# A hybrid decoder layer on one core: inputs turned by the host layout, FFN 1 first, memory keys and values beside the cross-attention

## The reference

```python
h = rmsnorm(x, ffn1_norm);  x = x + 0.5 * swiglu(h, ffn1_w_gate, ffn1_w_up, ffn1_w_down)   # 2048 -> 5504 -> 2048
h = rmsnorm(x, mix_norm);   proj = h @ w_in          # latent attention and gated recurrence on its columns
x = x + concat([a, r]) @ w_out
h = rmsnorm(x, xattn_norm); m = rmsnorm(mem, mem_norm)
x = x + memory_xattn(h, m, xattn_w_q, xattn_w_kv, xattn_q_norm, xattn_k_norm, xattn_w_o)
h = rmsnorm(x, ffn2_norm);  x = x + 0.5 * swiglu(h, ffn2_w_gate, ffn2_w_up, ffn2_w_down)

def memory_xattn(h, m, w_q, w_kv, q_norm, k_norm, w_o):      # 4 heads of 128
    q = rmsnorm((h @ w_q) per head, q_norm)
    kv = (m @ w_kv) per head;  k = rmsnorm(first 128 columns, k_norm);  v = last 128 columns
    p = softmax(q @ k.T * 128 ** -0.5)
    return (p @ v) @ w_o
```

## Time and profile before

| | |
|---|---|
| median of 3 runs | 2006.64 us (2006.51 to 2006.73) |
| profiled execution, first to last instruction (its span) | 2003.2 us; the profile gives no other time of its own |
| median less span: what lies around the instructions | 3.4 us |
| PE busy / DVE / ACT / POOL | 98% / 50% / 42% / 5% of the span |
| weight slots through `w_hi` | 341 |
| data moved | 357.89 MB, 179 GB/s on the mean |
| mean granted TensorE clock | 0.995 of full speed |

### The profile page before, as it was taken

One profiled execution on the slowest core, in us unless ns is written; L12 is line 12 of the kernel. 1 busy time (PEld: TensorE's weight loads), 2 busy tenths in 40 slices (PEclk: granted clock), 3 DMA queues, 4 the chain that ended last, 5 costly groups with the idle time before them and its releaser, 6 DMA issues. The chain is left out here.

```text
span 2003.2 us, 21967 instructions
## 1 busy us (share of the span) xinstructions
PE 1955.2 (98%) x9138; PEld 1635.0 (82%) x9138; DVE 999.3 (50%) x784; ACT 850.3 (42%) x795; POOL 100.1 (5%) x79
## 2 busy tenths in 40 slices
PE   7999999999999999999998998999999999999999
PEld 6888888888888988898886776788888888888987
DVE  4644444444444455475656564544444444444443
ACT  5533333333333334554546445444333333433332
POOL 0100000000000000150324000000000000000000
PEclk9999999999999999999999998999999999999999
DMA  8555555555555655555543353355555555555653
GB/s 311 168 191 190 189 190 189 191 197 194 189 188 163 210 179 184 158 168 168 168 147 107 104 168 126 113 192 190 190 190 191 191 191 189 190 189 173 198 190 131
DMA packets 182430, 357.89 MB, mean 179 GB/s; under 512 B 6500, under 2 KB 17111, under 8 KB 182103
## 3 DMA queue, kind: packets, MB, share of 16 engines
q1 hardware_dynamic: 182358, 356.88, 54.4%
HBM read 354.76 MB, written 2.10 MB: 178 GB/s over the span
## 5 line engine op out<-in xcount | busy, mean ns | idle before, releaser
L875 DVE TENSOR_TENSOR w_lo<-w_raw,w_hi 128x2048 fp32r<-128x2048 f32 (+1 forms) x341 | 772.7, 2266 | 911.1 <-ACT w_hi L524 910.0
L524 ACT ACTIVATE w_hi<-w_raw 128x2048 fp32r<-128x2048 f32 (+1 forms) x341 | 640.6, 1879 | 1011.9 <-PE acc L1370 1011.4
L1368 PE MATMUL acc<-w_hi,hT_hi 128*128 128x512 f32 (+2 forms) x1760 | 680.0, 386 | 0.8 <-DVE w_lo L875 0.8
L1370 PE MATMUL acc<-w_lo,hT_hi 128*128 128x512 f32 (+2 forms) x1760 | 675.8, 384 | 0.0
L1369 PE MATMUL acc<-w_hi,hT_lo 128*128 128x512 f32 (+2 forms) x1760 | 675.3, 384 | 0.0
L1368 PEld LDWEIGHTS acc<-w_hi,hT_hi 128*128 128x128 f32 x1760 | 330.5, 188 | 64.5 <-issue 3.2
L1370 PEld LDWEIGHTS acc<-w_lo,hT_hi 128*128 128x128 f32 x1760 | 330.4, 188 | 63.0
L1369 PEld LDWEIGHTS acc<-w_hi,hT_lo 128*128 128x128 f32 x1760 | 330.6, 188 | 61.0
L1368 PE MATMUL acc<-w_hi,actT_hi 128*128 128x512 f32 x752 | 295.5, 393 | 4.7 <-DVE w_lo L875 4.7
L1370 PE MATMUL acc<-w_lo,actT_hi 128*128 128x512 f32 x752 | 293.3, 390 | 0.0
L1369 PE MATMUL acc<-w_hi,actT_lo 128*128 128x512 f32 x752 | 293.3, 390 | 0.0
(11 more groups left out here) (204 smaller groups left out, 907.0 us busy)
## 6 DMA issues: line engine op xcount, KB each, us to landing
w_raw<-in_ffn_w_gate SPq DMA_DIRECT2D x80, 1024.0 KB, 5.1
w_raw<-in_ffn_w_up SPq DMA_DIRECT2D x80, 1024.0 KB, 5.1
w_raw<-in_ffn_w_down SPq DMA_DIRECT2D x80, 1024.0 KB, 5.2
w_raw<-in_w_in SPq DMA_DIRECT2D x36, 1024.0 KB, 5.1
w_raw<-in_w_out SPq DMA_DIRECT2D x16, 1024.0 KB, 5.2
w_raw<-in_xattn_w_kv SPq DMA_DIRECT2D x8, 1024.0 KB, 11.4
w_raw<-in_ffn_w_gate SPq DMA_DIRECT2D x8, 768.0 KB, 4.4
w_raw<-in_ffn_w_up SPq DMA_DIRECT2D x8, 768.0 KB, 4.4
```

Source lines behind the costliest of these rows:

```text
L524: nc.scalar.activation(w_hi[:, c % SPLIT, 0:n], raw[:, c % RAW, 0:n], ACT.Copy).then_inc(hi_done, 1)
L875: v.tensor_tensor(w_lo[:, c % SPLIT, 0:n], raw[:, c % RAW, 0:n], w_hi[:, c % SPLIT, 0:n].bitcast(F32), ALU.subtract).then_inc(lo_done, 1)
L1368: mm(dst, xh, wh, start=first and kk == 0, stop=False)
L1370: ins = mm(dst, xh, wl, start=False, stop=last and kk == tiles - 1)
```

## The change

- The host lays out more: `x` and `mem` come turned as well (`x_turned`, `mem_turned`), the norm gains as columns (`gain_columns`), and `xattn_w_kv` as two weights, keys (`xattn_w_k`) and values (`xattn_w_v`). PE no longer turns `mem`, `x` and the gains; ACT and DVE make the two parts straight from the loaded data.
- FFN 1 comes first. Its first slot is loaded, split and multiplied in four pieces of one k-tile (`first_slots`, `first_piece`).
- The 8 slots on the memory move: 4 key slots (`mem_k`) ahead of `w_q`, where they now take the place between which the norm of `x` is worked off; 4 value slots (`mem_v`) between the steps of the cross-attention. `mem` turned is loaded in two halves into one buffer (`load_memT`), which SP does in the midst of the loads of `w_out`, and split behind M5 and M7 (`mem_turned`).
- In the cross-attention the second scaling of the queries is gone: their 1/rms goes into the exponential's scale and the maxima, and POOL multiplies once more.
- The angles and bounds and the square sums of `mem` move into FFN 1's first down product.

```diff
@@ SP
+            def load_first():
+                sp.dma_start(gains[:, 0:N_ROWS], a["gain_columns"]).then_inc(gains_in, 16)
+                for k in range(4):
+                    sp.dma_start(xT[:, k, :], a["x_turned"][:, k, :]).then_inc(xT_in[k], 16)
+                    sp.dma_start(raw[:, 0, k * NW:(k + 1) * NW], wg[k * P:(k + 1) * P, 0:NW]).then_inc(first_in[k], 16)
+                for s in range(1, 4):
+                    sp.dma_start(xT[:, 4 * s:4 * s + 4, :], a["x_turned"][:, 4 * s:4 * s + 4, :]).then_inc(xT_in[3 + s], 16)
+                    load(s, 0, rows_of(wg, 4 * s, 4, slice(0, NW)), 4, NW)
...
+                        if n == "w_out" and j == 2 and s == 0:
+                            sp.wait_ge(ev("o_scaled"), 1)
+                            load_memT(0)
+                        if n == "w_out" and j == 3 and s == 0:
+                            sp.wait_ge(m_lo, KD // 2)
+                            load_memT(1)
                         load(slots[n] + 2 * j + s, 0, rows_of(a["w_out"][0], k0 + 4 * s, 4, slice(j * NW, (j + 1) * NW)), 4, NW)
-            for s in range(4):
-                load(slots["xq"] + s, 0, rows_of(a["xattn_w_q"][0], 4 * s, 4, slice(0, NW)), 4, NW)
+            for n, w in (("mem_k", a["xattn_w_k"]), ("xq", a["xattn_w_q"][0]), ("mem_v", a["xattn_w_v"])):
+                for s in range(4):
+                    load(slots[n] + s, 0, rows_of(w, 4 * s, 4, slice(0, NW)), 4, NW)
@@ ACT and DVE, behind M5 and M7 (ACT: hi and mT_hi; DVE: lo, add_block and mT_lo)
+                if k in (5, 7):
+                    mem_turned(k // 2 - 2)
@@ ACT
             for s in range(4):
                 hi(slots["xq"] + s, 0, 4, NW)
                 if s == 0:
+                    take(blocks["mem_k"], slots["mem_k"] + 4, lambda t: memk_nat[:, t, :], ACT.Copy, cols(rsq, "mem"))
+            turned(memkT, 0, groups["memk"], gain=col["xattn_k_norm"])
+            hi(slots["mem_v"], 0, 4, NW)
...
+            x_exps(0)
+            hi(slots["mem_v"] + 2, 0, 4, NW)
+            x_prob_turned(0)
+            x_exps(1)
+            hi(slots["mem_v"] + 3, 0, 4, NW)
+            x_prob_turned(1)
+            hi(slots["w_o"], 0, 4, NW)
+            take(blocks["mem_v"], slots["mem_v"] + 4, lambda t: memv[:, t, :], ACT.Copy, cols(rsq, "mem"))
+            hi(slots["w_o"] + 1, 0, 4, NW)
@@ DVE
+            x_shift(0)
+            lo(slots["mem_v"] + 2, 0, 4, NW)
+            x_shift(1)
+            lo(slots["mem_v"] + 3, 0, 4, NW)
             for p in range(XH // 2):
                 dve.wait_ge(ev("x_exps"), p + 1)
                 done(v.reciprocal(srec[:, p, :], ssum[:, p, :]))
+            lo(slots["w_o"], 0, 4, NW)
+            lo(slots["w_o"] + 1, 0, 4, NW)
             done.wait()
@@ PE
+            values_slot(0)
+            pe.wait_ge(ev("xq_raw"), TT)
+            turn_features(groups["xq"], 0, of(gate))
+            values_slot(1)
+            split_stands(groups["xq"])
+            x_scores(0)
+            values_slot(2)
+            x_scores(1)
+            x_probs(0)
+            values_slot(3)
+            x_probs(1)
+            stands(blocks["mem_v"])
```

More of the change, by code:

```diff
@@ L380, in load_memkv @@
[L380 to L392, removed]
@@ L508, in _ @@
             norm("k")
-            for name in ("o_mla", "x3", "xq", "x4"):
+            for name in ("o_mla", "x3", "memk"):
                 norm(name)
+            norm("xq", X_SCALE)
+            norm("x4")
         @block.scalar
@@ L552, in square_sums @@
                     done.wait()
-                    ins = nc.scalar.activation(flat_stage[:, 0:src.shape[2]], src[:, t, :], ACT.Square, accum_out=cols(sums, name, t, 1))
+                    junk = flat_stage[:, 0:src.shape[2]] if name != "mem" else src[:, t, :]
+                    ins = nc.scalar.activation(junk, src[:, t, :], ACT.Square, accum_out=cols(sums, name, t, 1))
                     if t == 0:
@@ L601, in pair @@
                         ins.then_inc(acc_taken[b0 % 2], 1)
-                        if not prev and h == 0 and f == 1:
-                            turned(memkT, 0, groups["memk"], gain=col["xattn_k_norm"])
-                        hi(c + 6, rep, 4, width)
-                        hi(c + 7, rep, 4, width)
+                        if not first:
+                            hi(c + 6, rep, 4, width)
+                            hi(c + 7, rep, 4, width)
                     pair(0, 0)
@@ L850, in _, with x_prob_turned @@
                 act.sem_inc(ev("x_exps"), 1)
-            for p in range(XH // 2):
+            def x_prob_turned(p):
                 for t in range(TT):
@@ new lines, in x_turned, with mem_turned @@
+            def x_turned(k):
+                c = col["ffn1_norm"] + k
+                dve.wait_ge(x_hi, k + 1)
+                v.scalar_tensor_tensor(hT_lo[:, k, :], xT[:, k, :], gains[:, c:c + 1], hT_hi[:, k, :].bitcast(F32),
+                                       ALU.mult, ALU.subtract).then_inc(x_lo, 1)
+            def mem_turned(half):
+                for k in range(KD // 2):
+                    c = half * KD // 2 + k
+                    g = col["mem_norm"] + c
+                    dve.wait_ge(m_hi, c + 1)
+                    v.scalar_tensor_tensor(mT_lo[:, c, :], memT[:, k, :], gains[:, g:g + 1], mT_hi[:, c, :].bitcast(F32),
+                                           ALU.mult, ALU.subtract).then_inc(m_lo, 1)
@@ L1288, in _ @@
                     turned_lo(hT_hi, hT_lo, 4 * (k // 2 - 2), groups["x_out"] + k // 2 - 2, 0, splits["x_out"] + k // 2 - 2, 0, gain=col["xattn_norm"])
+                if k in (5, 7):
+                    mem_turned(k // 2 - 2)
+            for s in range(4):
+                lo(slots["mem_k"] + s, 0, 4, NW)
+                if s == 0:
+                    turned_lo(hT_hi, hT_lo, 4 * (DB - 2), groups["x_out"] + DB - 2, 0, splits["x_out"] + DB - 2, 0, gain=col["xattn_norm"])
+                entry("x3", s, slots["mem_k"])
@@ L1355, in of, with slot @@
                 return lambda m, t: src[:, t, col0 + m * P:col0 + (m + 1) * P]
-            def slot(c, rep, B, lhs_hi, lhs_lo, k0, tiles, width, first, last, off=0, full=None, signal=True):
-                pe.wait_ge(lo_done, c + rep + 1)
+            def slot(c, rep, B, lhs_hi, lhs_lo, k0, tiles, width, first, last, off=0, full=None, signal=True, pieces=None):
+                if pieces is None:
+                    pe.wait_ge(lo_done, c + rep + 1)
                 full = full or width
                 for kk in range(tiles):
+                    if pieces is not None:
+                        pieces(kk)
                     w0 = kk * full + off
@@ L1642, in _ @@
                         turn_features(groups["x_out"] + j - 1, 0, of(x, (j - 1) * NW))
+            B = blocks["mem_k"]
+            free(B)
+            for s in range(4):
+                pe.wait_ge(m_lo, 4 * s + 4)
+                slot(slots["mem_k"] + s, 0, B, mT_hi, mT_lo, 4 * s, 4, NW, s == 0, s == 3)
+                entry("x3", s)
             B = blocks["xq"]
@@ L1648, in _, with values_slot, x_scores @@
                 slot(slots["xq"] + s, 0, B, hT_hi, hT_lo, 4 * s, 4, NW, s == 0, s == 3)
-                entry("x3", s)
-            pe.wait_ge(ev("xq_scaled"), 1)
-            turn_features(groups["xq"], 0, of(gate))
-            split_stands(groups["xq"])
-            for p in range(XH // 2):
+            pe.wait_ge(ev("memk"), 1)
+            turn_features(groups["memk"], 0, of(memk))
+            def values_slot(s):
+                B = blocks["mem_v"]
+                if s == 0:
+                    free(B)
+                slot(slots["mem_v"] + s, 0, B, mT_hi, mT_lo, 4 * s, 4, NW, s == 0, s == 3)
+            def x_scores(p):
                 for t in range(TT):
```

368 lines of the change are left out of this document (188 added, 180 removed).

## The result

| | before | after |
|---|---|---|
| median | 2006.68 us (2006.51 to 2006.96) | 2030.83 us (2028.9 to 2031.29) |
| ratio | | 1.012, interval 1.0107 to 1.0132 |
| span of the profiled execution | 2003.2 us | 2027.0 us |

The change costs 24 us. The prediction was 2022.6, range 2012 to 2030: the sign and all three waits were right, the size was 8 us short, and the time lies 0.8 us above the range.

The account below looks back on a forecast made before the run. PE, busy 98% of the span, was taken as the bound. Start -9.6, keys' turn -1.0, M6 +8.9, key slots +0.3, cross-attention +12.2, clock +5.2 sum to +16.0: span 2019.2, plus 3.4 gives 2022.6 us, range 2012 to 2030.

Parts of the forecast that it names:

- all three waits: Forecast case, chance 0.70: slower, with PE waiting at slot 1, before M6 and in the cross-attention.
- T to `w_o`: Cross-attention, end of fourth `w_q` slot to first `w_o` matmul: 61.3 us at full clock; 12.2 us lost.
- the clock's term: Waits of 8.9, 6.2 and 6.9 us before M6, v2, v3 each restart PE's clock: 3 x 1.75 = 5.2 us.
- With those of 5.1 and 3.8 it would be 8: Upper end for clock restarts: counting also the waits before v0 and the outputs, 8 us.
- the clock holds at 2.4 GHz: Rival, chance 0.08: PE's clock stays at 2.4 GHz through the waits, giving 2017 us.
- the value slots cover the waits: Rival, cross-attention at v2 and v3, chance 0.07: splits run under PE's previous slot, 12 us gained, 1995 us.
- SP's wait: Before M6: its load stands behind `mem`'s second half, which waits on `m_lo`; PE waits 8.9 us.
- not late: Rival before M6, chance 0.08: loads behind SP's wait are under way beside M5; no 8.9 us wait, 2012 us.
- Start: FFN 1's beginning: first matmul at 7.2 us, slot 1 at 17.7 after a 3.3 us wait; gain 9.6 us.
- Slot 1 4 us later: FFN 1's start: if the 1.6 MB in pieces moved at 200 GB/s, slot 1 some 4 us later, sum +20.
- the rival of slow pieces: FFN 1's start, chance 0.07: pieces load at 278 GB/s instead of 390, 8.3 instead of 5.9 us; 2025 us.
- The 3.4 us: Whole run: difference between span and median, added to the predicted span of 2019.2 to give 2022.6 us.

Follow-up runs that it names:

- idle matmuls in all five waits: Changed kernel with unused matmuls on PE in the waits before M6, v0, v2, v3 and the outputs: 2024.3 us, ratio 1.0093.
- the reordering: Changed kernel with ACT's and DVE's splits of v0, v2, v3 and `w_o` slots put ahead of the softmax steps: 1998.38 us, ratio 0.9965.
- both repairs: Changed kernel with `mem`'s second half loaded behind M7 and splits of v0, v2, v3, `w_o`'s first slot ahead of softmax steps: 1988.96 us.

## Why the prediction was right in kind and short in size

Its positions can be laid beside the trace: before M6 it had -54.6 us, the trace -52.6; M6 10.65, the trace 10.6; T to `w_o` 64.8 (61.3 and two restarts), the trace 70.8. Of the 7.8 us that its sum of +16.0 falls short of the span's +23.8, 2.0 lie ahead of M6 and 6.0 between T and `w_o`; smaller terms take 0.2 off. That M6 came out to 0.1 us is partly luck: its restart was put 0.3 us too short (1.75 for 2.1) and its wait as much too long.

**The step that failed is the clock's term**, "three restarts, 3 x 1.75 = 5.2": 4.9 of the 7.8 us. The run with idle matmuls in all five waits gives 10.1 for M6 and the cross-attention: 2.1 (10.6 less 8.5) and 8.0 (70.8 less 62.8). Two things were wrong in the term.

- The number of restarts, 3.7 us. The waits of 5.1 us before v0 and 3.7 before the outputs cost one too: 1.9 (13.58 less the 11.68 with idle matmuls) and 1.8 (16.33 us from probabilities' turn to `w_o`, 1262.49 to 1278.82, and 14.56 with idle matmuls, 1257.84 to 1272.40). The term took the 5 idle us of the earlier trace rows as what a fall needs, but these were one case, not a least length; and 5.1 is over 5, so by its own words v0's wait belonged in it.
- The size of one, 1.2 us over the three. M6's is 2.1, v2's and v3's 4.35 together, where 1.75 each was put down: behind M6 the ten matmuls from 1149.10 to 1153.42 took 4.3 us, 2.0 more than ten at 0.23. The 1.75 was "up to half" of one stretch at the program's start.

"With those of 5.1 and 3.8 it would be 8" stood there as the upper end and was nearer: the forecast would have been 2025.4. The rival "the clock holds at 2.4 GHz" is out.

**Cross-attention.** At full clock T to `w_o` is 62.8 (61.3 predicted): v0 at 6.2 from T (6.0), v2 at 27.0 (26.2), v3 at 42.7 (41.4). Each softmax step is longer than it was reckoned: from the first scores to the rounding of v2 it is 4.6 us (1227.97 to 1232.55), not 3.9. The mechanism, the value slot's split in line behind the step that it should cover, is shown by the reordering alone. It also shows the rival "the value slots cover the waits" to be a matter of order: with the splits first T to `w_o` is 38.3 (37 in the rival), and the case then comes out on the other side.

**SP's wait.** 8.77 us for 8.9, by the steps named: 52.6 us put back on, DVE's parts end at 1189.5 (1189.6 predicted), ACT gets the weight at 1197.3 (1197.5) and M6 begins at 1201.7 (1201.7). The rival "not late" is out.

**Start.** PE's first matmul and slot 1 came within 0.1 and 0.9 us. Slot 0 lost 2.8 and not 1.75 us to the lower clock (14 matmuls in the 6.05 us to 13.34, 3.2 at 0.23), which cost nothing, as slot 1 is bound by its load; it only made the wait shorter. By 12.0 us 2.90 MB had arrived (135, 277, 194, 326, 312, 302 and 386 GB/s in windows of 1.5 us from 1.5 on), where the earlier trace rows gave 3.2. At the last rate the 0.3 missing are 0.9 us, in line with ACT having slot 1's data at 14.18 and not 13.5. "Slot 1 4 us later", which the prediction worked out from the Trainium skill, DMA: Bandwidth & Descriptors, section Bandwidth, is out, and so is the rival of slow pieces with its 2.4: the four 128 KB and four 256 KB loads, issued one close behind the other, cost less than either. What was missed is that the wait before slot 1 mostly costs a restart. Of the predicted gain, 10.6 with the keys' turn, the profiled execution has 10.0, the other runs without idle matmuls there 8.0 to 9.2.

**Between FFN 1 and M6** 1.0 us was lost, in the stretch of the mixer's attention, whose instructions the change doesn't touch; in the other profiled executions it is -0.2 to 3.0. No run was made for it, but the traces show where it goes: to falls of the clock. In all eleven after the change the granted clock falls once at 1010 to 1013 us. The ledger then stands at -0.2 in the two with no other fall. It stands at 0.9 to 1.0 in the three that have one more, at 1030 to 1034, and at 2.6 to 3.0 in the six that have a third, at 1086 to 1088. The third follows a wait of PE that is 2.2 us long in every one of the eleven, and where it comes the matmuls behind that wait are 0.43 us apart and not 0.23. The windows of both places, first of the run with `mem`'s half behind M7 (2.9), then of that with both repairs (-0.2):

```profile
1029.00:1038.00 9.00, 6.85 (x30) 5.40 (x29) 3.97 (x6) 6.24 (x18) 3.11 (x2) 0.81 0.37 117
1085.00:1093.00 8.00, 5.83 (x25) 5.18 (x26) 3.53 (x8) 2.42 (x10) 0.00 (x0) 0.79 0.39 131
```

```profile
1029.00:1038.00 9.00, 6.86 (x39) 5.55 (x38) 3.99 (x6) 6.75 (x21) 3.11 (x2) 1.00 0.35 117
1085.00:1093.00 8.00, 6.87 (x36) 5.91 (x37) 2.44 (x8) 1.37 (x8) 0.00 (x0) 1.00 0.40 131
```

**Open.** What makes the clock fall in one execution and not in another, with the same wait, no run here settles. These falls limit what a median can say: the executions of one kernel differ by up to 5.6 us (the splits ahead, 1995.85 to 2001.42).

**The 3.4 us** between span and median, which the sum used, aren't what lies around the instructions, as the table before the prediction has it: no run shows that much there. The profiled execution of the changed kernel took 2028.9 us with a span of 2027.0, 1.9 more, and in the ten other runs it is 1.8 to 2.1. The rest was the difference between the execution that was profiled and the median one. It hardly touches the forecast, as the changed kernel's profiled execution is 1.9 us under its median too.

## What to carry to other kernels

Work put between the steps of a chain covers them only if its own preparation stands ahead of those steps in every engine's list; here the same instructions cost 22 us in one order and gained 10.4 against the kernel before in another. A load issued behind a wait delays every load behind it on that queue, so it belongs behind those that are needed sooner. Price a new wait of PE as its length plus a restart of the clock, 2 us in this kernel, also when it is only 3 or 4 us long, and read the price from the matmuls behind a wait, not from the program's start.

## What the runs showed of the hardware

- Waits of PE of 3.7 and 5.1 us were followed by work at 1.2 GHz, as those of 7 and 8.8 us were, and in eight of nine cases those of 2.6 to 4.2 us before slot 1. A wait of 2.2 us in the attention was followed by it in six of eleven executions. What makes a short wait go one way or the other was not varied.
- The price of a restart isn't fixed: v2 and v3 together took 1.3 us less in one execution than in another, with no change there. The Trainium skill, TensorE: Matmul & The Clock Gate, section What's actually happening, says that the number of matmuls that run at the low clock at a kernel's start differs from run to run. The traces agree: in the ten executions with the same pieces at the start it is 7 (both repairs) to 14 (the changed kernel).
- Idle matmuls hold the clock (1.00 in the windows of all the filled waits but the last), and the work behind them was not late for it: v0 begins 6.1 us behind the start of the keys' turn with them and 6.2 without, v2 15.2 behind the queries' turn either way. But where another wait follows, the fall can move there: at the outputs 1.8 us were saved and 1.4 paid at `w_o`. They are worth it only where the wait itself can't be removed: all five together gave 5.6 us by the medians, the reordering 31.5.
